# Three edits to small matmuls in a two-block decoder kernel: the scan's segment product, the modulation turn and the compression product

## Time and profile before

| | |
|---|---|
| Median of 3 runs | 2557.09 us (2555.96 to 2564.01) |
| Span of the profiled execution, first to last instruction | 2556.1 us |
| Lowest of the runs, 0.1 us under that span | 2555.96 us |
| PE busy | 2511.6 us, 98% |
| DVE, ACT, POOL busy | 1094.9, 927.1, 175.9 us |
| Time in the mixers' compression (line 1225), each of two | 7.1 us |
| Scan units | about 1285 to 1427 us |

### The profile page before, as it was taken

One profiled execution on the slowest core, in us unless ns is written; L12 is line 12 of the kernel. 1 busy time (PEld: TensorE's weight loads), 2 busy tenths in 40 slices (PEclk: granted clock), 3 DMA queues, 4 the chain that ended last, 5 costly groups with the idle time before them and its releaser, 6 DMA issues.

```text
span 2556.1 us, 32570 instructions
## 1 busy us (share of the span) xinstructions
PE 2511.6 (98%) x13272; PEld 1680.7 (66%) x13272; DVE 1094.9 (43%) x1678; ACT 927.1 (36%) x1451; POOL 175.9 (7%) x156
## 2 busy tenths in 40 slices
PE   7999999999999999999999999999999999999998
PEld 6888778888887788898967788444444444444443
DVE  5545575555554655567866545211111111111111
ACT  5435464444354554466644543111111111111111
POOL 1000300000002000042600000000000000000000
PEclk9999999999999999999999999999999999999999
DMA  7546665555556665433522346899999999999995
GB/s 259 188 165 216 236 226 193 181 192 193 183 203 215 240 226 183 150 133 133 172 76 99 111 148 249 346 425 430 432 431 431 431 431 431 432 432 431 432 431 254
DMA packets 69246, 688.21 MB, mean 269 GB/s; under 512 B 7890, under 2 KB 8034, under 8 KB 11776
## 3 DMA queue, kind: packets, MB, share of 16 engines
q1 hardware_dynamic: 66224, 676.01, 67.8%
q0 software_dynamic: 2928, 10.88, 1.2%
HBM read 683.72 MB, written 1.05 MB: 268 GB/s over the span
## 4 chain that ended last, share of the span: by engine, by line
PE 92%; DVE 4%; ACT 3%; issue 1%; DMA 0%; POOL 0%; SPq 0%; ACTq 0%; DVEq 0%
PE bank L443 39%; PE bank L2935 26%; PE bank L2882 5%; PE bank L1903 4%; PE bank L2949 3%; PE bank L2925 2%; PE bank L481 1%; ACT split_r L398 1%; DVE ring_r L409 1%; PE bank L2303 1%; DVE work L1961 1%; PE bank L1295 1%; PE bank L762 1%; PE bank L2288 1%; PE bank L1097 1%
## 5 line engine op out<-in xcount | busy, mean ns | idle before, releaser
L409 DVE TENSOR_TENSOR ring_r<-ring,split_r 128x2048 fp32r<-128x2048 f32 (+1 forms) x211 | 476.8, 2284 | 349.3 <-ACT split_r L398 349.1
L443 PE MATMUL bank<-split_r,xT_r 128*128 128x512 f32 (+1 forms) x1760 | 546.2, 388 | 4.5 <-DVE ring_r L409 3.0
L398 ACT CAST split_r<-ring 128x2048 fp32r<-128x2048 f32 (+1 forms) x228 | 429.1, 1905 | 159.3 <-PE bank L443 120.3
L443 PEld LDWEIGHTS bank<-split_r,xT_r 128*128 128x128 f32 x1760 | 328.7, 188 | 72.9 <-issue 7.2
L2935 PE MATMUL bank<-ring,work 128*64 128x512 f32 x1536 | 344.7, 598 | 1.7 <-issue 1.7
L443 PE MATMUL bank<-ring_r,xT_r 128*128 128x512 f32 (+1 forms) x880 | 339.3, 386 | 0.0
L443 PE MATMUL bank<-split_r,work_r 128*128 128x512 f32 x960 | 300.8, 391 | 0.5 <-DVE ring_r L409 0.5
L2935 PEld LDWEIGHTS bank<-ring,work 128*64 128x64 f32 x1536 | 107.6, 138 | 230.9 <-issue 230.9
L2935 PE MATMUL bank<-split,work 128*64 128x512 f32 x1024 | 232.2, 595 | 0.0
L443 PEld LDWEIGHTS bank<-split_r,work_r 128*128 128x128 f32 x960 | 180.3, 188 | 37.9 <-DVE ring_r L409 0.9
L2972 ACT ACTIVATE work<-work 128x512 f32<-128x512 f32 x32 | 20.1, 629 | 470.1 <-DVE work L2983 470.1
(11 more groups left out here) (394 smaller groups left out, 2959.0 us busy)
## 6 DMA issues: line engine op xcount, KB each, us to landing
ring<-in_stream SPq DMA_DIRECT2D x256, 1024.0 KB, 5.2
ring<-in_stream SPq DMA_DIRECT2D x96, 2048.0 KB, 13.9
split<-in_stream SPq DMA_DIRECT2D x64, 2048.0 KB, 12.0
work<-in_stream SPq DMA_DIRECT2D x32, 2048.0 KB, 11.2
row<-in_rows POOLq DMA_DIRECT2D x6, 512.0 KB, 4.3
ring<-in_stream SPq DMA_DIRECT2D x4, 560.0 KB, 4.6
work<-in_conv POOLq DMA_DIRECT2D x2, 768.0 KB, 5.6
x<-in_x SPq DMA_DIRECT2D x1, 1024.0 KB, 10.0
```

The lines of the kernel that those rows point to most:

```text
L398: act.copy(hi, self.part(half, self.ring)).then_inc(*up("half_hi", half.h))
L409: dve.tensor_tensor(self.part(half, self.ring_lo), self.part(half, self.ring), hi.bitcast(F32), ALU.subtract).then_inc(*up("half_lo", half.h))
L443: mm = self.nc.tensor.matmul(out, a[x][a_at], w[y][w_at], start=start and n == 0, stop=stop and n == 2)
```

## The change

1. **Scan.** The segment product's stationary column is cut from a wider constant (8 columns, one for each chunk and group, zero in the rows of the other chunk) and runs over all 128 rows in place of 64.
2. **Modulation.** Each 128-column part of `modp` is turned by a plain transpose (128 x 128, one record) instead of the product with `two_rows` (two records). DVE adds the four strips with a new `tensor_reduce` (`mod_summed`), waits for it, and adds the bias.
3. **Compression.** Even and odd steps write different strips, so that four strips are in use; each strip sums 8 steps. ACT copies the 128 rows out without the gelu. The turn is now a float32 product with a constant of 128 x 64 (`two_halves`), which adds the strip pairs. ACT applies the gelu after the turn (`cmp_gelu`), between the copy-out of `pe_bg(0)` and its part of unit 1, and DVE waits for that. The constants of the first block shrink from 466 to 400 columns.

```
-                mm = pe.matmul(bank[6][32 * kv:32 * kv + 32, 0:CMP_HIDDEN],
-                               self.xb[kv][:, j].rearrange("p a b -> p (a b)"), w[:, j, :], start=(j == 0), stop=(j == 15))
+                strip = 64 * (j % 2) + 32 * kv
+                mm = pe.matmul(bank[6][strip:strip + 32, 0:CMP_HIDDEN],
+                               self.xb[kv][:, j].rearrange("p a b -> p (a b)"), w[:, j, :], start=(j < 2), stop=(j >= 14))
...
-            tr = pe.transpose(self.bank[7][:, hb * 64:(hb + 1) * 64], self.hid_c[0:64, hb * P:(hb + 1) * P],
-                              self.ident[0:64, 0:64])
+            tr = pe.matmul(self.bank[7][:, hb * 64:(hb + 1) * 64], self.hid_c[:, hb * P:(hb + 1) * P],
+                           self.const("two_halves"), start=True, stop=True)
...
-            mm = pe.matmul(bank[7][:, 2 * k:2 * k + 2], self.modp[:, k * P:(k + 1) * P], self.const("two_rows"),
-                           start=True, stop=True)
-        mm.then_inc(*up("mod_turned", c))
+            tr = pe.transpose(bank[7][:, k * P:(k + 1) * P], self.modp[:, k * P:(k + 1) * P], self.ident)
+        tr.then_inc(*up("mod_turned", c))
...
+        part = self.att[:, 160:168].rearrange("p (k s) -> p k s", s=2)
+        strips = self.bank[7][:, :].rearrange("p (k j r) -> p k r j", k=4, j=4)[:, :, 0:2, :]
         dve.wait_ge(*at("mod_turned", c))
-        dve.tensor_tensor(self.mod_T.rearrange("p a k s -> p (a k) s")[:, 4 * c:4 * c + 4, :],
-                          self.bank[7][:, 0:8].rearrange("p (k s) -> p k s", s=2), spread(b, 2, 2),
+        dve.tensor_reduce(part, strips, AX.X, ALU.add).then_inc(*up("mod_summed", c))
+        dve.wait_ge(*at("mod_summed", c))
+        dve.tensor_tensor(self.mod_T.rearrange("p a k s -> p (a k) s")[:, 4 * c:4 * c + 4, :], part, spread(b, 2, 2),
                           ALU.add).then_inc(*up("mod_added", c))
...
-        act.activation(self.hid_c[0:64, :], bank[6][0:64, 0:CMP_HIDDEN], ACT.Gelu_apprx_tanh).then_inc(*up("cmp_hid", st))
+        act.copy(self.hid_c, bank[6][:, 0:CMP_HIDDEN]).then_inc(*up("cmp_hid", st))
...
                 self.act_evac(st, 5, self.bg, i, 7)
+                if i == 0:
+                    act.wait_ge(*at("cmp_turned", st))
+                    act.activation(self.hid_c[:, 0:P], bank[7][:, 0:P], ACT.Gelu_apprx_tanh).then_inc(*up("cmp_gelu", st))
...
-        dve.wait_ge(*at("cmp_turned", st))
-        hv = self.bank[7][:, 0:128].rearrange("p (hb a n) -> p hb a n", hb=2, a=4)
+        dve.wait_ge(*at("cmp_gelu", st))
+        hv = self.hid_c[:, 0:P].rearrange("p (hb a n) -> p hb a n", hb=2, a=4)
...
-            rows = slice(64 * m, 64 * m + 64)
-            pe.matmul(bank[2 + half][:, :].rearrange("p (h l) -> p h l", h=4), self.group_r[rows, g:g + 1].broadcast_to([64, P]),
-                      self.acs_wide[d][rows, 4 * half:4 * half + 4], start=False, stop=True).then_inc(*up("seg", u, half))
+            mg = m * NG2 + g
+            pe.matmul(bank[2 + half][:, :].rearrange("p (h l) -> p h l", h=4), self.group_r[:, mg:mg + 1].broadcast_to([P, P]),
+                      self.acs_wide[d][:, 4 * half:4 * half + 4], start=False, stop=True).then_inc(*up("seg", u, half))
```

More of the change, by code:

```diff
@@ L56 @@
 SHARED = {name: sem for sem, names in {
-    "mixer_dve": "angle rotated dup u xb cmp_hidT cmp_vb cmp_s cmp_step cmp_sub cmp_p conv att_step mod_copied mod_added att_sum cmp_added u_scaled o_scaled",
+    "mixer_dve": "angle rotated dup u xb cmp_hidT cmp_vb cmp_s cmp_step cmp_sub cmp_p conv att_step mod_copied mod_summed mod_added att_sum cmp_added u_scaled o_scaled",
     "mixer_pe": "cmp_turned cmp_kv cmp_scores cmp_p_turned cmp_o mod_turned xc_first bg_first",
-    "mixer_act": "rope cmp_hid gates cmp_exp cmp_pT cmp_o_out kT kc2 qT",
+    "mixer_act": "rope cmp_hid cmp_gelu gates cmp_exp cmp_pT cmp_o_out kT kc2 qT",
     "second_dve": "mod_T tap cx_lo acs_lo acs_wide dt xw_c xw h1 h_decayed decay yo y_sum y z_mul AB_even uT_lo y_lo hx_lo g0 gated mix mix_lo o_gained",
@@ L156, in constants @@
     i = np.arange(P)
-    q = np.arange(SEQ)
     c = {}
     c["ident"] = np.eye(P)
-    c["causal"] = np.where(q[None, :] <= i[:, None] + P, 0.0, NEG)
+    c["causal"] = np.where(i[None, :] <= i[:, None], 0.0, NEG)
     end = np.arange(NCP) * CMP_STRIDE + CMP_BLOCK - 1
@@ L168, in constants @@
     c["inv_freq"] = np.tile(inv.astype(np.float32)[None, :], (P, 1))
-    c["two_rows"] = (i[:, None] % 32 == np.arange(2)[None, :]).astype(np.float32)
+    c["two_halves"] = (i[:, None] % 64 == np.arange(64)[None, :]).astype(np.float32)
     return c
@@ L180, in constants_2 @@
     c["head_of"] = (i[:, None] % 8 == np.arange(8)[None, :]).astype(np.float32)
-    c["group_of"] = (i[:, None] % NH2 // 8 == np.arange(NG2)[None, :]).astype(np.float32)
+    mg = np.arange(MT * NG2)[None, :]
+    c["group_of"] = ((i[:, None] // 64 == mg // NG2) & (i[:, None] % NH2 // 8 == mg % NG2)).astype(np.float32)
     c["before"] = (i[:, None] < i[None, :]).astype(np.float32)
@@ L827, in act_ffn @@
                 act.copy(self.causal_r[:, 0:P], self.ident)
-                act.copy(self.causal_r[:, P:2 * P], self.const("causal")[:, P:2 * P]).then_inc(*up("causal", 0))
+                act.copy(self.causal_r[:, P:2 * P], self.const("causal")).then_inc(*up("causal", 0))
             if self.last_ffn and i == 2:
@@ L1724, in second_views @@
         self.gain1, self.gain2 = w(at + 3 * P, 2, KD), w(at + 3 * P + 2 * KD, KD)
-        self.group_r = wr(at + 3 * P + 3 * KD, NG2)
+        self.group_r = wr(at + 3 * P + 3 * KD, MT * NG2)
         self.base = 3072
-        assert at + 3 * KD + 3 * P + NG2 <= self.base
+        assert at + 3 * KD + 3 * P + MT * NG2 <= self.base
         self.acs_T = wr(12288, 2, P)
```

## The result

The changed kernel took 2544.27 us (median of 6, 2542.22 to 2551.28) against 2558.27 for the kernel before on the same chip (6 runs): ratio 0.9946, 95% interval 0.9932 to 0.9960. Two more measurements of it gave 0.9956 (0.9944 to 0.9969) and 0.9953 (0.9939 to 0.9967). So it is faster by 0.5%, some 12.5 us. The forecast was 2551.6 us, "the same" likelier than "faster", and a range from 2544.5: the direction of the sum was right, its size less than half.

The account below looks back on a forecast made before the run. PE, busy 98% of the span, was taken to bound the kernel. Scan -8.4, modulation -2.0, compression's turn +0.5 and clock +4.4 made -5.5 from 2556.1: span 2550.6, median 2551.6 us, range 2544.5 to 2556.5.

Parts of the forecast that it names:

- the clock's term: Gaps behind the compression, both layers: waits grown to 4.7 us drop the clock to half, 2.2 us each, +4.4.
- -9.9: Whole kernel without clock effects: scan -8.4, modulation -2.0, compression's turn +0.5.
- Scan, -8.4: Scan: 12.8 us of row-change cost removed, less 2.5 and 1.2 for `xw`, 0.6 at the gates, 0.1 in unit 0.
- Modulation, -2.0: Both mixers: 1.0 us saved each; turns 0, 2, 3, 5 save 0.37 each, turn 1 nothing, reduction costs 0.25.
- Turn 4: Modulation turn directly before the product awaiting its sum: 0.1 gained, but it begins behind a DVE chain some 0.3 longer.
- Compression, 0: Compression: product 3.5 us shorter, but none arrives; PE's wait for the second low half grows to 4.7 in both layers.
- the cover: PE's wait for the second low half behind the compression; without it the edit would be worth 3.5 a layer.
- B: Gaps behind the compression: the clock keeps up there, so -9.9, 2547.2 us, faster; chance 0.23.
- C: Scan and modulation: `xw` and the gates' half in time, reduction hidden, -12.3, 2544.8 us, faster; chance 0.12.
- D: Modulation: transposes don't hold the clock, two more spells a mixer, 13.6 us, 2565.2 us, slower; chance 0.05.
- E: Compression: its saving arrives because the split comes forward too, -9.9 - 7.0, 2540.2 us; chance 0.04.
- F: Scan: the broadcast constant's weight load isn't taken early anyway, so no gain there, 2560.0 us; chance 0.04.

Follow-up runs that it names:

- The modulation edit: Only the modulation's plain transposes and reduction, in the kernel before; ratio 0.9968 of before, and 0.9977 when run again.
- the scan alone: Only the scan's segment product over all 128 rows, in the kernel before; ratio 0.9966 of before, mean span 2549.2 us against 2558.2.
- before with its halves' waits taken apart: Kernel before, TensorE waiting for the second low half of W_bg only where it is used, not for both first; ratio 0.9979 of before.
- the five filling products: Changed kernel plus five discarded 128x512 identity products in TensorE's wait behind the compression; ratio 0.9941 of before.
- the run with the halves: Changed kernel, TensorE waiting for the second low half of W_bg only where it is used, not for both first; ratio 0.9927 of before.
- the earlier `xw`: Changed kernel with VectorE's next-unit `xw` issued before its wait for this unit's diagonal product; ratio 0.9940 of before.

## Why the prediction was wrong

**Where it failed: the clock's term, +4.4.** The forecast added the two new spells to an execution whose other spells it took as fixed. The added ones were real: 3.8 us by filling them. But other spells that before's profile had were missing or shorter in the changed kernel's, and that had no term. A 6.8 us spell in a mixer costs 2.86: before's two profiles need 41.18 and 38.32 us for the modulation stretch of the first mixer, with and without it. The modulation edit, forecast at -2.0, measured -6.8 (mean spans), of which its instructions explain 3.1 (below); the other 3.7 go with a higher clock, for which length and added transposes are ruled out as the reason and the two-column products are only a candidate. The router's spell (3.97 us of the profiled execution) is in both of before's profiles and in none of the changed kernel's three, and no run here says why. Taken together the mean clock of the changed kernel, 0.9957, is about before's 0.9959, where +4.4 us had it fall.

**The sum at full clock held.** -9.9 was forecast. The profile's -11.4 contains, by clock, +1.78 and +2.34 in the gaps, -1.2 in the first mixer (2.86 of loss becomes 38.86 - 37.22 = 1.64, against the second mixer, which had no spell) and -3.97 in the router, together -1.1 where +4.4 was forecast; so -10.3 at full clock.

**Scan, -8.4:** -7.4 in the profile, -8.9 in the mean of the scan alone, whose clock was a little higher (0.9960 against 0.9954). The price of a row change (0.2), its place in the weight load and the 0.23 of the wider product were right. `xw` cost 3.9 where 2.5 + 1.2 was forecast. Too small was unit 0: its diagonal product waits 1.0 us where before waited 0.5, not 0.1 more; and the gates take the 0.6 back as forecast (8.0 becomes 7.4). These make up 0.6 of the 1.0 that was missing; where the rest went isn't shown.

**Modulation, -2.0:** at full clock -3.1. The modulation stretch takes 37.22 us (second mixer of after) against 38.32 (second of before), 1.1 less; behind it the last turn and the second half of the projection give 0.4 to 0.5 more. A turn takes 0.36 where 0.44 was forecast, so each saves 0.45 and not 0.37; the reduction adds 0.22 for 0.25. Turn 1's saving is eaten as forecast, PE waiting for `mod_T`:

```profile
311.08 1.50 PE L1296 MATMUL bank<-ring,cs 128*32 128x512 f32 x12 [1.33 <-DVE mod_T L1330]
```

Two terms were mis-sized. Turn 4 was to lose 0.2 and gained 0.3: in the second mixer the product that waits for its sum comes 1.10 us sooner than before's, counted from the compressed keys (35.37 against 36.47), and what stands ahead of the turn 0.76 sooner. And a wait for a VectorE copy, which had no term, takes 0.4 a mixer of what turns 0, 2 and 3 bring:

```profile
324.79 1.10 PE L1097 MATMUL bank<-work 128*128 128x64 f32 x8 [0.43 <-DVE work L1589]
```

**Compression, 0:** right, to the wait of 4.66 for 4.7. The turn and the gelu, +0.5, came to nothing that can be seen (29.09 against 29.09 above). What the prediction says of the cover is wrong in one point: with that wait out of the way the edit would not be worth 3.5 a layer but 0.1, since other waits stand behind it. And the reading that the clock stays up through 1.5 us of idle time holds for before's two profiles, not for all.

**Rivals.** B and C named 2547.2 and 2544.8, near the result, by luck, since their reasons don't hold: the clock did fall in the gaps, and `xw` was late. D, by the Trainium skill (TensorE: Matmul & The Clock Gate, Part 4), had transposes as what lets the clock down; here the kernel with transposes in place of two-column products has the higher mean clock (0.9974 against 0.9959). Transposes added to those products didn't raise it either (0.9963 against 0.9961). E falls: the split took 5.56 us for 5.57 and did not come forward. F falls, by the 0.23 of the four products.

**The odds.** Half a range of C was cut at 2544.5, 0.2 us above the median. More to the point, the range had no case in which existing spells of the clock change, though the earlier trace rows showed one mixer with and one without.

## What to carry to other kernels

Stretches at half clock come and go between executions and between versions of a kernel: list every one in the profile of before, the router's too, give each a term with both signs, and look at it in more than one profile. A wait for all parts of an operand can be taken apart (0.9956 to 0.9927 here), but look past it before counting on a saving upstream: behind it further waits kept all but 0.1 us of 3.4. Idle TensorE time can be filled with discarded products for its clock alone (0.9956 to 0.9941) if their price is known first. The list of waits was a lower bound for what a late operand cost: 1.7 us listed, 3.9 gained.

## What the runs showed that was not expected

- The kernel with the modulation edit has a higher clock, 0.9974 against 0.9959, and keeps it at 0.9973 when its turns are made as long as before's: 4 us of 2558 that its instructions don't explain. That the two-column products do it is not shown; before with its halves' waits taken apart has them, and 0.9971.
- The half clock costs less than half its length where TensorE also waits: 6.8 us that begin in the first gap delay what follows by 1.78 us, 6.8 us in a mixer by 2.86, 10.2 us in the router by 3.97.
- VectorE's second subtraction goes with GpSimd's start. The two of L409 in the first layer took 5.57 us in before and 5.56 after, and the second alone 3.36 and 3.35. It took 2.3 with the five filling products: there GpSimd's tensor operations began at 268.77, just after that subtraction (268.72). In the first layer of the run with the halves it was the same (268.84 after 268.49), and with the earlier `xw` too (268.65 after 268.22). In the other thirteen profiles that recorded it GpSimd began first, and it took 3.35 to 3.37. With the five products `pe_bg(0)` started 10.61 us behind the compression in place of 11.37, which the clock has no part in:

```profile
266.51 4.49 DVE L409 TENSOR_TENSOR ring_r<-ring,split_r 128x2048 fp32r<-128x2048 f32 x2 [4.03 <-ACT split_r L398]
...
268.77 8.35 POOL L1693 TENSOR_TENSOR work<-work 128x512 f32<-128x512 f32 x5 [6.93 <-DMA work<-work]
```

- A 128x512 float32 product of the identity takes 0.82 us (nine in 7.42), in two records.
